# A split-precision down projection as seven half-size products, with the weight differences made two stages earlier

## The reference, cut to what matters

```
def ffn_sublayer(h, prev, g, w_gu, conv_w, conv_b, w_down):
    gate, up = jnp.split(rms_norm(h, g) @ w_gu, 2, axis=-1)
    gate_c, state = causal_dwconv3(gate, prev, conv_w)
    return h + (jax.nn.silu(gate_c + conv_b) * up) @ w_down, state
```

## Time and profile before

| what | before |
|---|---|
| device time, median of 3 runs | 1823.1 us (1813.66 to 1824.73) |
| the profiled execution: device time | 1823.89 us |
| its span, first to last instruction | 1822.1 us |
| PE busy | 1681.8 us, 92% of the span |
| DVE, ACT, POOL busy | 1112.3, 811.9, 732.7 us |
| the chain that ended last, by engine | PE 70%, DVE 15%, ACT 7%, issue 4%, POOL 2%, DMA 2% |
| mean granted TensorE clock | 0.949 of full speed |

### The profile page before, as it was taken

How to read it: one execution, slowest core, us unless ns; L and a number is a source line. 1 busy time by engine, 2 the same in 40 slices (tenths; PEclk the granted TensorE clock), 3 DMA queues, 4 the chain that set the end, 5 groups by cost and what they waited for, 6 DMA issues and landing times.

```text
span 1822.1 us, 34225 instructions
## 1 busy us (share of the span) xinstructions
PE 1681.8 (92%) x13965; PEld 1179.9 (65%) x14043; DVE 1112.3 (61%) x1906; ACT 811.9 (45%) x1483; POOL 732.7 (40%) x704
## 2 busy tenths in 40 slices
PE   6999999997776889989979997999999999999998
PEld 3644444444444665445568654788888888898897
DVE  5856665788797875356745337888888878500000
ACT  5455478754533774342356325544444444301100
POOL 3232266888440110320033516666666666502200
PEclk9998899999787999989977999999999999999999
DMA  7031112122424110301253312112112112312311
GB/s 234 14 106 56 36 36 69 48 70 98 148 84 142 54 48 1 113 1 35 73 159 119 105 41 93 47 47 70 48 47 71 47 47 87 117 43 92 99 41 29
DMA packets 136550, 132.78 MB, mean 73 GB/s; under 512 B 15358, under 2 KB 109630, under 8 KB 136356
## 3 DMA queue, kind: packets, MB, share of 16 engines
q1 hardware_dynamic: 123850, 118.79, 21.1%
q10 hardware_dynamic: 12544, 11.80, 2.1%
HBM read 114.58 MB, written 15.98 MB: 72 GB/s over the span
## 4 chain that ended last, share of the span: by engine, by line
PE 70%; DVE 15%; ACT 7%; issue 4%; POOL 2%; DMA 2%; SPq 0%; ACTq 0%; DVEq 0%; POOLq 0%
PE PS L1611 23%; PE PS L1664 4%; PE PS L1665 4%; PE PS L1666 4%; PE PS L958 4%; PE PS L959 4%; PE PS L960 3%; ACT arena L1703 2%; PE PS L1155 2%; PE PS L1153 2%; ACT arena L1764 2%; PE PS L1154 2%; PE PS L1311 2%; PE PS L1323 1%; DVE arena L432 1%
## 5 line engine op out<-in xcount | busy, mean ns | idle before, releaser
L1611 PE MATMUL PS<-arena 128*128 128x272 f16 (+1 forms) x3696 | 429.9, 280 | 5.0 <-issue 5.0
L1611 PEld LDWEIGHTS PS<-arena 128*128 128x128 f16 (+1 forms) x3696 | 362.3, 98 | 72.8 <-issue 5.4
L1703 ACT ACTIVATE arena<-PS 128x512 f16<-128x512 f32 (+10 forms) x354 | 175.0, 523 | 176.6 <-PE PS L1323 41.4
L368 POOL TENSOR_TENSOR arena<-arena 128x512 bf16<-128x512 f32 (+2 forms) x144 | 161.3, 1154 | 189.8 <-ACT arena L359 189.5
L1703 ACT ACTIVATE arena<-arena 128x512 f16<-128x512 f32 (+5 forms) x214 | 136.0, 657 | 225.2 <-PE PS L1611 117.3
L958 PE MATMUL PS<-arena 128*128 128x512 f16 (+2 forms) x584 | 204.6, 361 | 8.1 <-POOL arena L368 3.5
L959 PE MATMUL PS<-arena 128*128 128x512 f16 (+2 forms) x584 | 204.3, 361 | 0.0
L1664 PE MATMUL PS<-arena 128*128 128x256 f16 x704 | 191.9, 273 | 1.4 <-POOL arena L936 1.0
L1665 PE MATMUL PS<-arena 128*128 128x256 f16 x704 | 191.9, 273 | 0.0
L1666 PE MATMUL PS<-arena 128*128 128x256 bf16 x704 | 191.9, 273 | 0.0
L960 PE MATMUL PS<-arena 128*128 128x512 bf16 (+2 forms) x544 | 188.0, 357 | 0.0
(11 more groups left out here) (363 smaller groups left out, 3777.8 us busy)
## 6 DMA issues: line engine op xcount, KB each, us to landing
arena<-w_gu SPq DMA_DIRECT2D x44, 512.0 KB, 5.0
arena<-w_down SPq DMA_DIRECT2D x8, 1408.0 KB, 7.2
arena<-w_in SPq DMA_DIRECT2D x8, 1024.0 KB, 6.2
arena<-w_kv_mem SPq DMA_DIRECT2D x8, 1024.0 KB, 7.0
arena<-cache_mem_k SPq DMA_DIRECT2D x32, 256.0 KB, 3.6
arena<-cache_mem_v ACTq DMA_DIRECT2D x28, 256.0 KB, 5.0
arena<-w_in SPq DMA_DIRECT2D x24, 256.0 KB, 3.7
arena<-x_prompt SPq DMA_DIRECT2D x9, 512.0 KB, 6.4
```

Of the source, the lines that this page charges most:

```text
L368: x = e.tensor_tensor(self.low(n)[:, 4 * half + k, :], wst[half][:, k, 0:width], self.high(n)[:, 4 * half + k, :], ALU.subtract)
L1611: mm = e.matmul(PS[:, product_bank(f, i) + c, 0:TC], w[:, i, k], s[i][:, q, c, :], start=first, stop=last)
L1703: e.activation(out, in_, ACT.Copy, **kw).then_inc(sem(name), 1)
```

## The change

The core of the diff (the scratch views, the store helpers and semaphore offsets are left out):

```diff
+            def sum_load(k):
+                if k >= 2:
+                    e.wait_ge(sem("tw_lo"), upto("tw_lo", 4 * (k - 1)))
+                for kh in range(2):
+                    e.dma_start(tw_in[k % 2][:, kh, :, :].rearrange("p a b -> p (a b)"),
+                                w_down[(kh * KH + k) * P:(kh * KH + k + 1) * P, :]).then_inc(sem(f"tw_ld{k % 2}"), 16)
+            def sum_store(k):
+                e.wait_ge(sem("tw_lo"), upto("tw_lo", 4 * (k + 1)))
+                for to, x in zip(tw_dram, (tw_hi, tw_lo)):
+                    e.dma_start(to[:, :, k, :].rearrange("i p n -> p i n"), x[:, :, :]).then_inc(sem("tw_st"), 16)
...
+            def sum_hi(k):
+                if k == 0:
+                    e.wait_ge(sem("s2_mm"), NI1)
+                else:
+                    e.wait_ge(sem("tw_st"), upto("tw_st", 32 * k))
+                for q in range(4):
+                    e.wait_ge(sem("tw_sum"), upto("tw_sum", 4 * k + q + 1))
+                    copy(tw_hi[:, q, :], tw_in[k % 2][:, T_AT[q] // 2, T_AT[q] % 2, :], "tw_hi")
+            SUM_HI_AT = {4: 7, 7: 8, 9 + 5: 9, 18 + 5: 10}
...
+                if x in SUM_HI_AT:
+                    sum_hi(SUM_HI_AT[x])
...
             for f in range(NC_T):
                 A.split_lo(e, A_CONV + f + 1)
+                for k in ((6, 7), (8,), (9,), (10,))[f]:
+                    lows_of(k)
+                    if k + 1 < KH:
+                        sums_of(k + 1)
                 e.wait_ge(sem("s4_ev"), last_of[f] + 1)
...
+            for w in range(6):
+                first, steps = STEP_ENDS[w], STEP_ENDS[w + 1] - STEP_ENDS[w]
+                for k in range(KH):
+                    for n in range(first + steps * k // KH, first + steps * (k + 1) // KH):
+                        left_sum(n)
+                        if n > first or w in (2, 4):
+                            left_lo(n - 1)
+                    if k == KH - 1 and w in (0, 2, 4, 5):
+                        left_lo(STEP_ENDS[w + 1] - 1)
+                    if w > 0 and k in (4, 7, 9):
+                        down_sum(w, (4, 7, 9).index(k))
+                for t in range(0 if w == 0 else 3, 5 if w in SAMPLES else 4):
+                    down_sum(w, t)
+            for t in (4, 0, 1, 2, 3):
+                down_sum(P3, t)
```

More of the change, by code:

```diff
@@ new lines, in bank_used, with item_end, piece @@
+        def bank_used(n):
+            return max([m + 1 for m in range(n) if down_bank(*DOWN[m]) == down_bank(*DOWN[n])] or [0])
+        def item_end(i):
+            return max(n + 1 for n, it in enumerate(DOWN) if it[0] == i)
+        PIECES = [(i, k) for i in (P2, P3) for k in range(KH)]
+        W_BLOCK = {P2: (1, 0), P3: (1, 1)}
+        NPIECE = len(pieces)
+        T_AT = (0, 1, 3, 2)
+        TW = {P5: 0, P7: 1, P6: 2, P4: 3}
+        def piece(i, k):
+            return pieces[PIECES.index((i, k)) % NPIECE]
@@ L658, in memory_value_page, with piece_loaded, first_half @@
+        def piece_loaded(e, i, k):
+            x = PIECES.index((i, k))
+            e.wait_ge(sem(f"ws_ld{x % NPIECE}"), 16 * (x // NPIECE + 1))
+        STEPS = [(a, k) for a in range(4) for k in range(KH)]
+        STEP_ENDS = [0, 11, 17, 22, 28, 37, 44, 44]
+        def first_half(half):
+            return range(6) if half == 0 else range(6, KH)
         def memory_value_page(e, n):
@@ L906, in _ @@
-            down_store(e, DOWN_ENDS[3], ND2)
-            e.wait_ge(sem("ffnst_ev"), upto("ffnst_ev", 1))
+            for half in range(2):
+                e.wait_ge(sem("fw_sum"), upto("fw_sum", 5 * FT))
+                e.wait_ge(sem("fw_lo"), 7 * (FT - 1) + ((M5 if half == 0 else M7) + 1))
+                ks = first_half(half)
+                e.dma_start(dst[:, ks.start:ks.stop, :],
+                            w_down[ks.start * P:ks.stop * P, 0:512].rearrange("(k p) n -> p k n", p=P)
+                            ).then_inc(sem(f"dw_ld{half}"), 16)
@@ new lines, in down_tile @@
+            def down_tile(i, t, first):
+                (xh, xl), wh, wl, cols = LEFT[i], z_hi[i % 2], z_lo[i % 2], slice(t * P, (t + 1) * P)
+                out = PS[:, down_bank(i, t), :]
+                for k in range(KH):
+                    if first:
+                        left_ready(i, k)
+                        right_ready(i, k)
+                    e.matmul(out, xh[:, k, cols], wh[:, k, :], start=(k == 0 and i not in (P6, P7)), stop=False,
+                             skip_group_check=i in CHAIN)
+                    e.matmul(out, xl[:, k, cols], wh[:, k, :], start=False, stop=False, skip_group_check=i in CHAIN)
+                    mm = e.matmul(out, xh[:, k, cols], wl[:, k, :], start=False, stop=(k == KH - 1),
+                                  skip_group_check=i in CHAIN)
+                mm.then_inc(sem("sw_mm"), 1)
@@ new lines, in down_samples @@
+            def down_samples(i, first):
+                k0, wh, wl = SAMPLES[i][0], z_hi[i % 2], z_lo[i % 2]
+                for k in range(KH):
+                    if first:
+                        right_ready(i, k)
+                    for x, w in ((fs_hi, wh), (fs_lo, wh), (fs_hi, wl)):
+                        for g in range(2):
+                            mm = e.matmul(PS[g * NS:(g + 1) * NS, down_bank(i, 4), 0:256], x[:, k0 + k, :],
+                                          w[:, k, g * 256:(g + 1) * 256], start=(k == 0 and x is fs_hi and w is wh),
+                                          stop=(k == KH - 1 and w is wl))
+                mm.then_inc(sem("sw_mm"), 1)
@@ L1812, in _ @@
                     value_out(j)
+                for j in range(value_done(m - 5), value_done(m - 4)):
+                    if j % 2:
+                        sum_hi(j // 2)
                 if m == 8:
```

451 lines of the change are left out of this document (298 added, 153 removed).

## The result

| what | before | after |
|---|---|---|
| device time, median (4 runs each, side by side) | 1823.91 us | 1841.63 us (1837.7 to 1843.01) |
| ratio, 95% interval | | 1.0101 (1.0055 to 1.0148) |
| the profiled execution: device time, span | 1823.89, 1822.1 us | 1837.7, 1835.8 us |

The change costs 1.0%: 17.7 us by the medians, 13.7 by the two profiled spans. The prediction was 1824, its range 1803 to 1846, and its likeliest class "within 1%"; the result stands at the edge of that class (the interval of the ratio reaches to both sides of 1.01), 14 to 18 us above the predicted time.

What follows compares the result with a forecast made beforehand. PE was taken to bound the down product, POOL's last convolution turn to delay all behind it. Span 1822.1 + 31.6 (loop 22.6, scores 9) - 30.8 (down product, tail) = 1822.9; forecast 1824 us, range 1803 to 1846.

Steps and rivals of the forecast that it cites:

- within 1%: Whole kernel: time stays within about 1% (18 us), what a measurement can tell from no change; chance 0.6.
- The down product and the tail: Last stretch: 924 matmuls of 512 columns replace 2112 of 256; with a shorter end, -30.8 us in all.
- The two terms for waits: Down product's first product, P1: 0.5 us kept for POOL's low part, +2.5 for ACT's copy of the last transposes.
- the rival with 0.06: Down product: DVE ends its windows late and each product waits for its left side; 1849 us, chance 0.06.
- The loop: Convolution loop: POOL's turns f = 0 to 3 late by +8.4, +6.3, +6.3, +1.6; +22.6 us, between 18 and 32.
- the round trip through DRAM: Convolution loop: low parts are stored and must land before ACT's next copies; landing taken at 4.3 us, 3.0 to 7.2.
- The score and value stage: Front: POOL's sums and low parts slow DVE, and copies block ACT's relus; +9 us, between +3 and +15.
- The four blocks in ACT's relus: Score and value stage: four ACT copy blocks of 2.1 us among its relus cost +2 us.
- The delay was carried whole: From POOL's first rotary turn on: the front's +31.6 us is carried whole, or +28.6 if PE's lateness binds.
- the rival that hid it: Behind the convolution loop: the front's delay is taken up by POOL's later work; 1792 us if hidden whole, chance 0.18.
- the front costs more: Front: slow store landings, POOL and DVE slowing each other in loop and scores; +25, 1849 us, chance 0.16.
- The signs: Expected trace: POOL's convolution products near 240, 280, 319, 354; first rotary turn near 372; PE idle some 6 us before each f.

Runs made afterwards that it cites:

- experiment 5: Changed kernel, same order, but k = 5, 7 and 9 use a second pair of buffers so copies need not wait for the store just before: 1837.66 us.
- Experiment 4: Changed kernel with the same operations reordered in the convolution loop, POOL's and ACT's early work moved into their waits: 1821.16 us, ratio to the original 1.0005.
- experiment 2: Changed kernel with POOL's early work in the score and value stage (k = 0 to 3) shrunk to two 16-column operations per k: 1825.43 us.
- experiment 3: Changed kernel with ACT's four 512-wide copies per k in the score and value stage (k = 0 to 3) shrunk to one of 16 columns: 1839.2 us.
- e7_later: Changed kernel's operations with weight differences moved: k = 0, 1 to the sample stage, the rest beside output projection and memory queries: 1798.08 us, ratio to the original 0.9887.
- experiment 7: Changed kernel with POOL's 512-wide two-input operations in the score and value stage (k = 0 to 3) replaced by 1024-wide one-input copies: 1836.87 us.

## Why the prediction was right or wrong

**The down product and the tail: right.** Forecast -29.4 and -1.4, measured -29.6 and -1.1, and the kernel without early work gives it by itself (223.5 us from the first matmul to the end). The two terms for waits were off in opposite ways, 1.8 for 0.5 and 0.9 for 2.5; that their sum came near (2.7 for 3.0) is luck. No product after the first waited for DVE, so the rival with 0.06 is refuted.

**The loop: right in size.** Forecast +8.4, +6.3, +6.3, +1.6; measured +9.0, +6.8, +6.7, +1.3, and 2.4 more in the convolution of f = 3, where POOL waited 6.0 us for the taps behind a sign step, which I had not seen. Its mechanism was told one-sidedly. I made the turn long by the round trip through DRAM; but in after POOL's sums of k = 9, which my sum of the turn left out, end at 289.15 and the store lands at 289.0, and with the trip taken out (experiment 5) a turn still takes 38.5 us: that gives back 1.4 of 6.7. Two paths of equal length stood there, and I had seen one. Experiment 4 shows what the rest is: work in a row in front of the convolution, with room for it elsewhere in the same turn.

**The score and value stage: the term that was mis-sized.** It was +9, between +3 and +15, and 16.6 was measured, above its own upper end. The mechanism, DVE and POOL slowing each other, was the right one (experiment 2: 15.2 of the 16.6 go with POOL's share). The size was wrong mainly in one factor. "DVE's 52.5 us then grow by 0.5 of the overlapped half, about 15": POOL was busy 65.5 of 74 us, so nearly 0.9 of DVE's time was overlapped, and not half. 52.5 x 0.88 x 0.55 is 25; DVE's time for the stage grew by 28.6 (80.0 against 51.4), so the slowing was a little dearer too, about 0.6. Less the 9.5 us of idle time that it filled (21.4 us idle before, 11.9 after), DVE ended the stage 19.1 us later, and ACT's copy, which stands a little ahead of DVE's end, came 16.6 later. The next sentence of the prediction has the POOL time that shows it, 70 us at the shared pace "from 98 to some 168", which is POOL busy throughout, and I had not put it back into DVE's sum. The four blocks in ACT's relus, +2, cost 0.7 by the marks, or 1.6 from the stage's start (experiment 3).

**Between that stage and the fourth item: a term that was missing.** +3.6. Behind the stage ACT's `sum_hi(5)` waited 6.0 us for a landing in front of a sign step, and small DVE instructions of the sample stage took a microsecond each beside POOL's sums; I had cost nothing there. How the 3.6 divide no run shows.

**The delay was carried whole: right.** +46.4 at the first rotary turn, +44.2 at the first down matmul; the rival that hid it (0.18) is refuted. In eleven profiled executions with the same work there (all but e7_later), the stretch between these two marks took 1225.3 to 1231.6 us; of the same program, after, once 1225.3 and once 1228.4. So the 2 us between +46.4 and +44.2 are no gain by the change, and within those 6 us of spread the delay went through whole. The rival "the front costs more" named the contention rightly, but placed a part of it in the loop, where POOL's instructions took 1.13 us, not 1.9; its point of decision, a front of 49, was just missed.

**The signs.** POOL's products were to start near 240, 280, 319 and 354 and came 12 to 13 us later, all four; the waits in front of three of them ended with ACT (2.5, 2.5, 2.4 us), and ACT waited for a transfer, as told. PE waited for POOL's low weights 8.9 us in two waits and 6.5 in a third, where 6 each was told. DVE's additions of 1024 took 2.25 us, not 1.8.

In sum: front 46.4 where 31.6 stood, of the 14.8 between them 7.6 from the mis-sized term, 6.0 from the two that were missing, and 1.2 from the loop's sizes. The front was outside its own range of 23 to 45, and the time at the upper end of the likeliest case's own range, 1814 to 1842. It lies in the range given, 1803 to 1846, because the other half of the sum was right and that range was wider, not because the front was.

## What to carry to other kernels

Before work is put on an idle engine, take that engine's busy share with the new work in it, multiply the time of the neighbour's instructions that have both inputs in SBUF by it and by the slowing (about 0.6 here), and see whether the neighbour then passes the bound of the stage; and look for the stage where it can't, even far away. Work in a loop is worth placing gap by gap: the same instructions cost 6.7 us a turn in front of a wait and next to nothing inside the waits. A gain and a loss in one change are two questions; the run that leaves one of them out answers both.

## What the runs showed of the hardware

- POOL instructions on SBUF slow DVE instructions whose two tensor inputs are in SBUF by 1.5 to 1.8 (725 to 1061 ns, 736 to 1325, 1284 to 2250: means over a stretch in which POOL is busy most of the time), not the reduction (686 to 686) nor the subtraction out of PSUM (681 to 680). This bears out the rule cited in the prediction (the Trainium skill, "GPSIMD Engine Reference", "8. Key points") on DVE's side, and adds that POOL's own second input is not needed: 1024-wide copies with one input took 1403 ns each (two of 512 take 2 x 609) and did nearly the same harm (experiment 7).
- POOL pays too: four 512-wide subtractions took 4.5 us in the loop and up to 7.9 beside the widest additions of the scores.
- Small DVE instructions can be held a whole microsecond: conversions and integer operations of 3 or 6 columns that take 0.17 us took 1.07 to 1.24 beside POOL's sums (from 208.68 on in after).
- A 512 KB store in pieces of 1 KB landed 4.6 us after its issue as the second of a pair, 3.0 as the first (medians of 11). With the 0.4 us between the issues that is 5.0 for the pair, where the prediction had 4.3 from rows and 4.4 as its other estimate.
